# Moving modulation dot products from the retention heads into the later heads, the output projection and the first MLP group

## The chip, the cores and the metric

One core of a Trainium2 chip runs the kernel. The metric is the device time of one execution in microseconds (us), lower is better. Five engines take part: PE multiplies matrices, DVE and ACT work on tiles, POOL does small side work, and SP issues DMAs. Each engine runs its own instructions in order, and they meet through semaphores.

## What is computed

One decoder block for 512 tokens of width 2048, in float32. What matters here is `mod`, six vectors of 2048 that scale, shift and gate the activations. It is one row times a 2048 x 12288 matrix, and only `sh1` and `sc1` are needed by the first norm.

```python
def reference(x, c, w_ada, b_ada, norm1_w, norm2_w, w_in, ...):
    silu_c = jax.nn.silu(c)
    for l in range(DEPTH):
        mod = silu_c @ w_ada[l] + b_ada[l]
        sh1, sc1, g1, sh2, sc2, g2 = jnp.split(mod, 6, axis=-1)
        h = modulate(rms_norm(x, norm1_w[l]), sh1, sc1)
        proj = h @ w_in[l]
        rq, rk, rv, rg, dq, dk, dv = jnp.split(proj, split_pts, axis=-1)
        ...   # 8 retention heads make y_ret, 8 differential heads make y_dif
        mixed = jnp.concatenate([y_ret, y_dif], axis=-1).astype(x.dtype) @ w_out[l]
        x = x + g1[:, None, :] * mixed
        h2 = modulate(rms_norm(x, norm2_w[l]), sh2, sc2)
        mlp = jnp.square(jax.nn.relu(h2 @ w_mlp1[l])) @ w_mlp2[l]
        x = x + g2[:, None, :] * mlp
    return rms_norm(x, final_norm_w)
```

## The kernel before

All matrix products run on PE in a split form. A **chunk** is 8 weight blocks of 128 x 128, 512 KB in all. SP loads it from HBM into one of 4 `raw` slots. ACT rounds it into `w_hi` (`round_w`), DVE makes the rest `w_lo = raw - w_hi` (`rest_w`), both in 2 slots, and PE runs 24 matmuls of 512 columns (`split_products`): 16 with `w_hi`, then 8 with `w_lo`. ACT may write `w_hi` of chunk s when PE has finished chunk s-2 (`chunk_done`), SP may load chunk s when `rest_w` of chunk s-4 is done (`lo_ready`).

The stages, in order:

- The first norm, with the 64 dot products that it needs, and 16 chunks of the input projection.
- Retention heads. Phase h projects head h, and beside that finishes head h-1. Phases 1 to 4 and 8 have 6 chunks, phases 5 to 7 have 8. Phase 8 already loads the first differential head.
- Differential phases 9 to 15 with 6 chunks each. The last head is finished beside the first 8 chunks of the output projection.
- The output projection: tiles m = 0 to 3 together in 8 chunks, then tiles 4 to 15 with 2 chunks each. After each tile DVE adds it to `xy` (`residual_out`) and sums squares.
- The second norm, and 8 MLP groups of 32 chunks: 16 "up" chunks (8 tiles, 2 chunks each) and 16 "down" chunks. In group 0 the first four up tiles share chunks 0 to 7 of the group, up tile 4 is chunks 8 and 9, up tile 5 is chunks 10 and 11, and so on; the down chunks are 16 to 31.

The dot products of `mod` run on DVE. One output column of 128 takes two dots of 128 x 1024, one for each half of `silu_c` (`dot_ada`, line 873). Each needs a 512 KB row block of `ada`, which SP loads into a ring of four slots of `ada_sb` when the dot four before is done (`load_ada`, line 323). In before, the 128 dots that the first norm does not need stand in the eight retention phases, 16 in each: `ADA_6` and `ADA_8` say how many pairs follow the `rest_w` of each chunk j of the phase. At a phase's end `modulation_sum` (lines 1065 and 1070) adds the halves and writes 8 columns of `modr`. `modr` has four rows of 16 columns: gate 1 (used from the output projection's first `residual_out`), shift 2 and scale 2 (used at the second norm), gate 2 (used by the `residual` of the MLP's down tiles).

Nothing plans the order: what each engine does is written out by hand, and SP's queue is one list in which a DMA that has to wait holds up all that stand behind it.

Of the kernel before, what the change touches and what calls it, by code (L numbers as in the profile page):

```python
# [152 lines left out]
def block_kernel(nc, x_t, c, ada, weights, vecs, lams, rot, decay, ident_in, mask_in, out):  # L153
    with ExitStack() as ctx:
        def sb(name, shape, dt=F32):
            return ctx.enter_context(nc.sbuf_tensor(name, shape, dt))
# [100 lines left out]
        relu = sb("relu", [P128, 2, TOK])  # L257
        usq = sb("usq", [P128, 2, TOK])

        bank = [ctx.enter_context(nc.psum_tensor(f"bank{i}", [P128, TOK], F32)) for i in range(8)]  # L260
# [6 lines left out]
        raw_landed = [sem(f"raw_landed{i}") for i in range(NRAW)]  # L267
        ada_landed = [sem(f"ada_landed{i}") for i in range(NADA_1)]
        x_landed = [sem(f"x_landed{i}") for i in range(KT // 2)]
        hi_ready, lo_ready, chunk_done = sem("hi_ready"), sem("lo_ready"), sem("chunk_done")  # L270
# [37 lines left out]
        def _(sp):  # L308
# [9 lines left out]
            def load_ada(a):  # L318
# [4 lines left out]
                sp.dma_start(ada_at(r), ada[a.value()]).then_inc(ada_landed[r], 16)  # L323

            def load_phase(h, s0, slots):

                part = 0
                for j in range(len(slots)):
                    load_raw(s0 + (j + 2))
                    for _ in range(2 * slots[j]):  # L330
                        load_ada(Count(A_RET - 16 + part, (16, h)) if not isinstance(h, int)
                                 else Count(A_RET - 16 + 16 * h + part))
                        part += 1
                    if j == 2 and (not isinstance(h, int) or h < NRET):
                        sp.wait_ge(strips_ready, h)
                        sp.dma_start(decay_sb[:], decay[h]).then_inc(decay_landed, 16)
# [18 lines left out]
            load_phase(NRET, Count(C_DIF), ADA_6)  # L355
            with sp.Fori(0, 10) as i:
                for j in range(4):
                    load_raw(Count(C_DIF + 8 + j, (4, i)))
            for s in range(C_OUT, C_OUT + 12):
                if s >= C_OUT + 4:  # L360
                    p = s - C_OUT - 4
                    sp.wait_ge(act_ready, KT + 2 * p + 2)
                    sp.dma_start(xy[:, 2 * p:2 * p + 2], x_t[:, 2 * p:2 * p + 2]).then_inc(x_landed[p], 16)
                load_raw(Count(s))
            with sp.Fori(0, (N_CHUNKS - C_OUT - 12) // 4) as i:
                for j in range(4):
                    load_raw(Count(C_OUT + 12 + j, (4, i)))
            for tb in range(TB):
# [493 lines left out]
        def _(dve):  # L862
# [198 lines left out]

            def modulation_sum(n, col):

                dve.wait_ge(dot_done, 16 * n + A_RET)
                nc.vector.tensor_tensor(sumr[:], partr[:, :, 0], partr[:, :, 1], ALU.add).then_inc(modr_summed, 1)
                dve.wait_ge(modr_summed, n)
                flat = modr[:].rearrange("p a b -> p (a b)")
                to = flat[:, bass.ds(col, 8)] if not isinstance(col, int) else flat[:, col:col + 8]
                bias = vec[:, bass.ds(col + V_B, 8)] if not isinstance(col, int) else vec[:, V_B + col:V_B + col + 8]
                nc.vector.tensor_tensor(to, sumr[:], bias, ALU.add).then_inc(modr_ready, 1)  # L1070

            def head_ret(h, s0, slots, dif=False):

                part = 0
                for j in range(len(slots)):
                    if j == 1:
                        means_of_v(h - 1)
                    rest_w(s0 + (j + 1))
                    if j == 0:
                        rest_v(h - 1)  # L1080
                    if j == 1:
                        if not isinstance(h, int) or h > 1:
                            finish_ret(h - 2)
                    if j == 2:
                        rotate_q(h, s0 + 2, dif)
                    if j == 4:
                        var_eps(h - 1)
                        rotate_k(h, s0 + 4, dif)
                    for _ in range(slots[j]):
                        a = Count(A_RET - 16 + 16 * h + 2 * part) if isinstance(h, int) else \  # L1090
                            Count(A_RET - 16 + 2 * part, (16, h))
                        modulation_rest(a, part)
                        part += 1
                    if j == 0:
                        decay_strips(h - 1)
                modulation_sum(h, 8 * h - 8)

            def head_dif(h, s0):

                for j in range(6):  # L1100
# [13 lines left out]
                    if j == 2:  # L1114
                        combine(h - 1)
                        rotate_q(h, s0 + 2, True)
                    if j == 4:
                        clamp_o(h - 1)
                        rotate_k(h, s0 + 4, True)
                    if j == 5:  # L1120
                        var_eps(h - 1)

            nc.vector.memset(ones[:], 1.0).then_inc(const_ready, 1)
# [55 lines left out]
            dve.wait_ge(modr_ready, NRET)  # L1179
            nc.vector.scalar_tensor_tensor(amul[:, 1], modr[:, 2], 1.0, vec[:, V_N2:V_N2 + KT], ALU.add, ALU.mult)\  # L1180
                .then_inc(scale_ready, 1)
            head_dif(NRET + 1, Count(C_DIF + 6))
# [55 lines left out]
            for g in range(1, 4):  # L1238
                for t in range(4):
                    for half in range(2 if (g, t) != (1, 0) else 1):  # L1240
                        rest_w(Count(C_OUT + 8 * g + 2 * t + half + (1 if (g, t) != (1, 0) else 2)))
                    m = 4 * g + t
                    residual_out(m, Count(C_OUT + 2 * m + 2))
                    sum_square(KT + m)
            token_mean(2)
            token_diag(2)
# [235 lines left out]
```

## Time and profile before

| | us |
|---|---|
| median of 3 runs | 2445.53 |
| lowest and highest | 2444.48 and 2446.52 |
| span of the profiled execution | 2444.3 |
| PE busy, of the span | 2337.2 |
| DVE busy, of the span | 1280.3 |
| ACT busy, of the span | 750.8 |

The page gives the profiled execution by its span alone; it lies 1.2 us under the median. PE is the engine that is nearly always busy, so the places to look at are those where it is not, or where its clock is down. [...]

### The profile page before, as it was taken

What the parts mean: (1) busy time and instruction counts of PE and PEld (TensorE: products, weight loads), DVE (VectorE), ACT (ScalarE), POOL (GpSimd) and SP (SyncE); (2) the same over time, 40 slices, a digit from 0 to 9 for tenths busy, and PEclk for the clock granted to TensorE, in tenths of its full rate; (3) what the DMA queues carried; (4) which work ended last, traced back from release to release, by engine and by line L of the source; (5) the groups of instructions that cost most, each with busy time, mean ns of one, the idle gap of its engine ahead of it and who ended that gap; (6) DMA issues with size and microseconds to landing.
All of it is one profiled execution on the core that took longest, in us unless ns stands there. A gap on an engine that the chain in (4) does not pass through costs nothing.

```text
span 2444.3 us, 28432 instructions
## 1 busy us (share of the span) xinstructions
PE 2337.2 (96%) x10284; PEld 1895.6 (78%) x10284; DVE 1280.3 (52%) x1752; ACT 750.8 (31%) x1014; POOL 185.0 (8%) x121
## 2 busy tenths in 40 slices
PE   4999999989999999899999999999999999999996
PEld 2567778877777778788888888888888888888885
DVE  7979999885666643443333333333333333333354
ACT  3233333434444532332222221221221221322332
POOL 0013233222122100000000000000000000000000
PEclk9999899999999999899999999999999999999998
DMA  9957777842222422222232223222222232222222
GB/s 369 384 208 272 264 263 263 281 161 77 78 77 69 137 95 94 78 95 95 95 103 95 94 97 100 94 94 96 101 95 94 95 101 97 94 94 99 94 91 86
DMA packets 98308, 328.22 MB, mean 134 GB/s; under 512 B 10064, under 2 KB 18768, under 8 KB 98128
## 3 DMA queue, kind: packets, MB, share of 16 engines
q1 hardware_dynamic: 97248, 326.41, 39.1%
q10 hardware_dynamic: 1008, 1.13, 0.1%
q8 instruction: 31, 0.51, 0.1%
q14 instruction: 21, 0.17, 0.0%
HBM read 323.31 MB, written 4.19 MB: 134 GB/s over the span
## 4 chain that ended last, share of the span: by engine, by line
issue 60%; PE 21%; DVE 12%; ACT 5%; DMA 0%; POOL 0%; DVEq 0%; ACTq 0%; POOLq 0%; SPq 0%
PE bank L389 6%; PE bank L390 6%; PE bank L393 6%; DVE ada_sb L873 4%; DVE w_lo L866 2%; ACT w_hi L621 2%; PE bank L496 1%; ACT prob L705 1%; DVE prob L873 1%; DVE bank L1020 1%; ACT L695 1%; PE bank L412 1%; DVE prob L1048 1%; PE bank L487 0%; ACT prob L688 0%
## 5 line engine op out<-in xcount | busy, mean ns | idle before, releaser
L389 PE MATMUL bank<-act_hi,w_hi 128*128 128x512 f32 x2112 | 842.1, 399 | 16.3 <-DVE act_lo L918 7.8
L390 PE MATMUL bank<-act_lo,w_hi 128*128 128x512 f32 x2112 | 832.7, 394 | 0.0
L866 DVE TENSOR_TENSOR w_lo<-raw,w_hi 128x1024 fp32r<-128x1024 f32 x392 | 495.2, 1263 | 400.9 <-ACT w_hi L621 386.3
L621 ACT ACTIVATE w_hi<-raw 128x1024 fp32r<-128x1024 f32 x392 | 414.3, 1057 | 924.5 <-PE bank L393 874.5
L393 PE MATMUL bank<-act_hi,w_lo 128*128 128x512 f32 x2112 | 521.8, 389 | 0.0
L389 PEld LDWEIGHTS bank<-act_hi,w_hi 128*128 128x128 f32 x2112 | 403.7, 191 | 109.6 <-issue 21.9
L390 PEld LDWEIGHTS bank<-act_lo,w_hi 128*128 128x128 f32 x2112 | 403.1, 191 | 85.0 <-issue 1.7
L393 PEld LDWEIGHTS bank<-act_hi,w_lo 128*128 128x128 f32 x2112 | 396.5, 188 | 82.5
L389 PE MATMUL bank<-u_hi,w_hi 128*128 128x512 f32 x1024 | 399.9, 390 | 0.0
L390 PE MATMUL bank<-u_lo,w_hi 128*128 128x512 f32 x1024 | 398.6, 389 | 0.0
L1227 DVE SCALAR_TENSOR_TENSOR xy<-bank,modr,xy 128x512 f32 (+1 forms) x144 | 108.1, 751 | 434.1 <-PE bank L393 434.1
L393 PE MATMUL bank<-u_hi,w_lo 128*128 128x512 f32 x1024 | 252.9, 389 | 0.0
L873 DVE CUSTOM_DVE_ANT_0 ada_sb<-ada_sb,silu_c 128x1024 f32<-128x1024 f32 x172 | 239.1, 1433 | 0.0
L393 PEld LDWEIGHTS bank<-u_hi,w_lo 128*128 128x128 f32 x1024 | 192.2, 188 | 39.9
L389 PEld LDWEIGHTS bank<-u_hi,w_hi 128*128 128x128 f32 x1024 | 192.3, 188 | 39.8
L390 PEld LDWEIGHTS bank<-u_lo,w_hi 128*128 128x128 f32 x1024 | 192.2, 188 | 39.7
L1262 DVE TENSOR_TENSOR usq<-relu 128x512 f32<-128x512 f32 x64 | 44.3, 692 | 235.2 <-ACT relu L820 235.2
L1318 POOL TENSOR_TENSOR tok_r<-tok_v,minus_half 128x4 f32<-128x4 f32 x3 | 3.9, 1293 | 1582.6 <-DVE tok_v L895 1582.6
L820 ACT ACTIVATE relu<-bank 128x512 f32<-128x512 f32 x64 | 38.2, 598 | 273.4 <-PE bank L393 273.4
L639 ACT ACTIVATE sq<-xy 128x512 f32<-128x512 f32 x48 | 30.1, 630 | 130.5 <-DVE xy L1227 125.9
L412 PE MATMUL bank<-xy,raw 128*128 128x512 f32 x128 | 56.8, 596 | 9.0 <-ACT xy L632 9.0
L1323 POOL TENSOR_TENSOR q_lo<-rot_a,q_hi 128x512 fp32r<-128x512 f32 x16 | 22.7, 1416 | 421.0 <-ACT q_hi L654 421.0
(130 smaller groups left out, 1224.1 us busy)
## 6 DMA issues: line engine op xcount, KB each, us to landing
raw<-weights SPq DMA_DIRECT2D x400, 512.0 KB, 3.3
ada_sb<-ada SPq DMA_DIRECT2D x172, 512.0 KB, 5.0
prob<-ada SPq DMA_DIRECT2D x20, 512.0 KB, 6.5
xy<-x_t SPq DMA_DIRECT2D x16, 512.0 KB, 5.9
out<-xy SPq DMA_DIRECT2D x4, 1024.0 KB, 9.1
decay_sb<-decay SPq DMA_DIRECT2D x7, 256.0 KB, 4.7
silu_c<-c_row SPq DMA_DIRECT2D x1, 1024.0 KB, 5.3
rot_sb<-rot ACTq DMA_DIRECT2D x2, 256.0 KB, 6.9
```

The source lines that it names most:

```text
L389: pe.matmul(acc[:], stationary, hi, start=first, stop=False)
L390: pe.matmul(acc[:], stationary, lo, start=False, stop=False)
L393: mm = pe.matmul(acc[:], w_lo[:, w, i * P128:(i + 1) * P128], hi, start=False, stop=last)
L412: mm = pe.matmul(bank[i][:], raw[:, k % NRAW, i * P128:(i + 1) * P128], xy[:, k], start=k == 0, stop=k == KT - 1)
L496: mm = pe.matmul(ps_a[:, jb * P128:], v_tok[:, jb], strips[:, STRIP[jb]:STRIP[jb] + TOK - jb * P128], start=(jb == 0), stop=(jb == TB - 1) ...
L621: nc.scalar.activation(w_hi[:, w], raw[:, r], ACT.Copy).then_inc(hi_ready, 1)
L639: nc.scalar.activation(sq[:, m % 2], xy[:, m % KT], ACT.Square).then_inc(sq_ready, 1)
L820: nc.scalar.activation(relu[:, t % 2], bank[t][:], ACT.Relu).then_inc(relu_ready, 1)
L866: nc.vector.tensor_tensor(w_lo[:, w], raw[:, r], w_hi[:, w].bitcast(F32), ALU.subtract).then_inc(lo_ready, 1)
L873: nc.vector.tensor_tensor_reduce(ada_at(r), ada_at(r), silu_c[:, half * HALF:(half + 1) * HALF], 1.0, 0.0, ALU.mult, ALU.add, to).then_inc ...
L1227: nc.vector.scalar_tensor_tensor(to, bank[t][:], gate_col, to, ALU.mult, ALU.add).then_inc(bank_free[t], 1)
L1262: nc.vector.tensor_tensor(usq[:, t % 2], relu[:, t % 2], relu[:, t % 2], ALU.mult).then_inc(usq_ready, 1)
```

## The change

Four dots in every phase from 1 to 15, two after chunk 3's `rest_w` and two after the last chunk's (60 dots; the sum at the end of each phase gives 2 columns). Four after each of the output projection's tiles 4 to 12 (36 dots, summed once at tile 13 with the 18 columns, where `amul` for the second norm is now made). The last 32, which make gate 2, use a ring of two slots `late` in the part of SBUF that the heads have left: four dots after each of the up tiles 4 to 7 of MLP group 0, and two after each of that group's first eight down tiles. `silu_c` is kept past the heads for it. SP's list changes to match: in the phases it loads 4 row blocks instead of 16, in the output projection four after every second chunk's load, and in MLP group 0 two behind each chunk load from chunk 9 on.

```diff
+A_UP = A_RET + 96
+NLATE = 2
+ADA_6 = (0, 0, 0, 1, 0, 1)
+ADA_8 = (0, 0, 0, 1, 0, 0, 0, 1)
...
+            def load_late(a):
+
+                r = ada_place(Count(a))[0]
+                if a < A_UP + NLATE:
+                    sp.wait_ge(o_done, NRET + NDIF)
+                else:
+                    sp.wait_ge(dot_done, a + 1 - NLATE)
+                sp.dma_start(late[:, r], ada[a]).then_inc(late_landed[r], 16)
...
+            for s in range(C_OUT + 2, C_OUT + 2 * KT):
...
                 load_raw(Count(s))
-            with sp.Fori(0, (N_CHUNKS - C_OUT - 12) // 4) as i:
+                m = (s - C_OUT - 4) // 2
+                if (s - C_OUT) % 2 == 0 and 4 <= m < 13:
+                    for e in range(4):
+                        load_ada(Count(A_RET + 60 + 4 * (m - 4) + e))
+            late_next = A_UP
+            for s in range(C_MLP, C_MLP + 28):
+                load_raw(Count(s))
+                if s >= C_MLP + 9 and late_next < N_ADA:
+                    for _ in range(2):
+                        load_late(late_next)
+                        late_next += 1
...
+            def modulation_late(col):
+
+                for e in range(2):
+                    a = A_UP + 2 * col + e
+                    r, landed = ada_place(Count(a))
+                    dve.wait_ge(late_landed[r], 16 * landed)
+                    nc.vector.tensor_tensor_reduce(late[:, r], late[:, r], silu_c[:, e * HALF:(e + 1) * HALF], 1.0, 0.0,
+                                                   ALU.mult, ALU.add, partr[:, col % 8, e:e + 1]).then_inc(dot_done, 1)
...
                     residual_out(m, Count(C_OUT + 2 * m + 2))
                     sum_square(KT + m)
+                    if m < 13:
+                        for e in range(2):
+                            modulation_rest(Count(A_RET + 60 + 4 * (m - 4) + 2 * e), 2 * (m - 4) + e)
...
-            up_quad(0, 1, Count(C_MLP + 8))
-            down_group(Count(C_MLP + 16))
+            for t in range(4):
+                for half in range(2):
+                    rest_w(Count(C_MLP + 9 + 2 * t + half))
+                rest_u(0, 4 + t, t)
+                modulation_late(2 * t)
+                modulation_late(2 * t + 1)
+            modulation_sum(NRET + NDIF + 1, 48, 8, A_UP + 16)
+            for m in range(KT):
+                rest_w(Count(C_MLP + 17 + m))
...
+                residual(3, m, m % 4, Count(C_MLP + 17 + m))
+                if m < 8:
+                    modulation_late(8 + m)
```

DVE at the end of retention phase 1, before: `rest_w` of the last chunk, four dots, the sum, then `rest_w` and `v_lo` (`rest_v`) of the next phase. An ISA row with `ada_sb` is a dot, the row `partr` behind it reads its sum.

```order
L866 TENSOR_TENSOR w_lo<-raw,w_hi 128x1024 [waits hi_ready]
L873 ISA ada_sb,partr<-ada_sb,silu_c 128x1024 [waits ada_landed0]
L873 ISA partr 128x1
L873 ISA ada_sb,partr<-ada_sb,silu_c 128x1024 [waits ada_landed1]
L873 ISA partr 128x1
L873 ISA ada_sb,partr<-ada_sb,silu_c 128x1024 [waits ada_landed2]
L873 ISA partr 128x1
L873 ISA ada_sb,partr<-ada_sb,silu_c 128x1024 [waits ada_landed3]
L873 ISA partr 128x1
L1065 TENSOR_TENSOR sumr<-partr 128x8 [waits dot_done]
L1070 TENSOR_TENSOR modr<-sumr,vec 128x8 [waits modr_summed]
L866 TENSOR_TENSOR w_lo<-raw,w_hi 128x1024 [waits hi_ready]
```

The same place after.

```order
L895 TENSOR_TENSOR w_lo<-raw,w_hi 128x1024 [waits hi_ready]
L902 ISA ada_sb,partr<-ada_sb,silu_c 128x1024 [waits ada_landed2]
L902 ISA partr 128x1
L902 ISA ada_sb,partr<-ada_sb,silu_c 128x1024 [waits ada_landed3]
L902 ISA partr 128x1
L1103 TENSOR_TENSOR sumr<-partr 128x2 [waits dot_done]
L1109 TENSOR_TENSOR modr<-sumr,vec 128x2 [waits modr_summed]
L895 TENSOR_TENSOR w_lo<-raw,w_hi 128x1024 [waits hi_ready]
L1000 TENSOR_TENSOR v_lo<-bank,v_hi 128x512 [waits v_hi_ready]
```

Two dots stand there instead of four. In MLP group 0 SP's queue was a loop of chunk loads that wait for `lo_ready` alone. After, from the output projection's last chunks on (the row with x13 ends with chunk 9 of the group), it is this list, in which the first pair of `late` is followed by chunk 10, the second by chunk 11, the third by chunk 12:

```order
L324 DMA raw<-weights 128x1024 [waits lo_ready] x13
L340 DMA late<-ada 128x1024 [waits o_done] x2
L324 DMA raw<-weights 128x1024 [waits lo_ready]
L340 DMA late<-ada 128x1024 [waits dot_done] x2
L324 DMA raw<-weights 128x1024 [waits lo_ready]
L340 DMA late<-ada 128x1024 [waits dot_done] x2
L324 DMA raw<-weights 128x1024 [waits lo_ready]
```

So from chunk 11 on every chunk load stands behind two loads that wait for dots. DVE in the same stretch, from the `rest_w` of chunks 9 and 10 on; `usq` and `u_lo` are `rest_u` of up tile 4, which waits until PE has finished chunk 9:

```order
L895 TENSOR_TENSOR w_lo<-raw,w_hi 128x1024 [waits hi_ready] x2
L1317 TENSOR_TENSOR usq<-relu 128x512 [waits relu_ready]
L1320 TENSOR_TENSOR u_lo<-usq,u_hi 128x512 [waits u_hi_ready,usq_ready]
L1097 ISA late,partr<-late,silu_c 128x1024 [waits late_landed0]
L1097 ISA partr 128x1
L1097 ISA late,partr<-late,silu_c 128x1024 [waits late_landed1]
L1097 ISA partr 128x1
L1097 ISA late,partr<-late,silu_c 128x1024 [waits late_landed0]
L1097 ISA partr 128x1
L1097 ISA late,partr<-late,silu_c 128x1024 [waits late_landed1]
L1097 ISA partr 128x1
L895 TENSOR_TENSOR w_lo<-raw,w_hi 128x1024 [waits hi_ready] x2
```

The first two dots that the second pair of loads waits for come behind `rest_u` of up tile 4; before, `rest_w` of chunk 11 stood there.

## Rows read from the trace of the kernel before

**Rows 1.** PE's waits for `v_lo`: us in total, times, longest us.

```profile
PE bank L441 <- DVE v_lo L971: 13.0, 5, 3.1
```

**Rows 2.** Stretches: length; busy PE, PEld, DVE, ACT, POOL; clock; DMA share; GB/s.

```profile
196.05:240.45 44.40, 41.25 (x176) 33.83 (x174) 42.08 (x59) 14.53 (x20) 13.46 (x8) 0.92 0.78 267
...
329.05:384.35 55.30, 52.17 (x224) 42.85 (x222) 48.42 (x67) 19.83 (x25) 15.01 (x8) 0.94 0.77 268
384.35:433.44 49.09, 49.09 (x223) 40.46 (x222) 44.64 (x61) 19.83 (x25) 13.30 (x7) 1.00 0.78 262
```

**Rows 3.** PE in order of time (start, us): the stall in phase 2.

```profile
201.21 0.47 PE L441 MATMUL bank<-ident_r,v_hi 128*128 128x128 f32 x1 [3.15 <-DVE v_lo L971]
```

**Rows 4.** DVE in order of time: third of four dots, then what PE waits for.

```profile
195.15 1.62 DVE L873 CUSTOM_DVE_ANT_0 ada_sb<-ada_sb,silu_c 128x1024 f32<-128x1024 f32 x1
...
199.34 1.22 DVE L866 TENSOR_TENSOR w_lo<-raw,w_hi 128x1024 fp32r<-128x1024 f32 x1
200.47 0.68 DVE L971 TENSOR_TENSOR v_lo<-bank,v_hi 128x512 fp32r<-128x512 f32 x1
```

**Rows 5.** Stretches from PE's resumption to the end of its lower clock.

```profile
149.14:152.60 3.46, 3.46 (x8) 2.71 (x9) 1.34 (x3) 2.78 (x4) 1.28 (x1) 0.51 1.02 398
201.21:207.20 5.99, 5.99 (x18) 5.12 (x19) 5.96 (x12) 1.14 (x4) 0.00 (x0) 0.50 1.01 402
...
529.35:534.85 5.50, 5.50 (x22) 4.51 (x23) 3.11 (x12) 2.71 (x8) 0.00 (x0) 0.50 0.20 61
```

**Rows 6.** DVE from phase 8's third last-chunk dot to phase 9's first maxima.

```profile
519.66 1.62 DVE L873 CUSTOM_DVE_ANT_0 ada_sb<-ada_sb,silu_c 128x1024 f32<-128x1024 f32 x1
...
524.04 1.22 DVE L866 TENSOR_TENSOR w_lo<-raw,w_hi 128x1024 fp32r<-128x1024 f32 x1
...
527.65 0.17 DVE L1026 TENSOR_SCALAR ntop<-top 128x4 f32<-128x4 f32 x1
```

**Rows 7.** PE at the second scores of phases 9 and 10.

```profile
529.35 0.58 PE L462 MATMUL bank<-k_hi,q_hi 64*128 64x256 f32 x2 [6.79 <-ACT prob L705]
...
573.32 0.39 PE L462 MATMUL bank<-k_hi,q_hi 64*128 64x256 f32 x2 [1.24 <-ACT prob L705]
```

**Rows 8.** DVE in a differential phase, behind the places of the new dots.

```profile
594.36 1.22 DVE L866 TENSOR_TENSOR w_lo<-raw,w_hi 128x1024 fp32r<-128x1024 f32 x1 [2.16 <-ACT w_hi L621]
...
608.86 1.47 DVE L866 TENSOR_TENSOR w_lo<-raw,w_hi 128x1024 fp32r<-128x1024 f32 x1 [5.02 <-ACT w_hi L621]
```

**Rows 9.** Output projection: one tile's two chunks on PE, then DVE in it.

```profile
897.89:908.77 10.88, 10.88 (x50) 9.01 (x49) 3.89 (x4) 2.64 (x3) 0.00 (x0) 1.00 0.29 96
...
900.55 1.22 DVE L866 TENSOR_TENSOR w_lo<-raw,w_hi 128x1024 fp32r<-128x1024 f32 x1 [0.26 <-ACT w_hi L621]
```

**Rows 10.** A dot on DVE, and SP's two loads that wait for it and the next.

```profile
159.54 1.22 DVE L873 CUSTOM_DVE_ANT_0 ada_sb<-ada_sb,silu_c 128x1024 f32<-128x1024 f32 x1
...
160.79 1.47 SPq L323 DMA_DIRECT2D ada_sb<-ada  x2
```

**Rows 11.** MLP group 0: PE starts chunk 10, DVE's `rest_u`, PE starts chunk 11.

```profile
1075.97 0.39 PE L389 MATMUL bank<-act_hi,w_hi 128*128 128x512 f32 x1
...
1077.54 0.69 DVE L1265 TENSOR_TENSOR u_lo<-usq,u_hi 128x512 fp32r<-128x512 f32 x1
...
1081.41 0.39 PE L389 MATMUL bank<-act_hi,w_hi 128*128 128x512 f32 x1
```

**Rows 12.** SP in phase 6: two dot loads and the chunk load behind them.

```profile
412.87 1.48 SPq L323 DMA_DIRECT2D ada_sb<-ada  x2
414.61 0.33 SPq L316 DMA_DIRECT2D raw<-weights  x1
```

**Rows 13.** Issue to landing, us: that chunk load, then one alone at 1079.81.

```profile
raw<-weights SPq DMA_DIRECT2D x1, 512.0 KB, 5.5
...
raw<-weights SPq DMA_DIRECT2D x1, 512.0 KB, 3.4
```

**Rows 14.** The page: `w_hi`'s group, busy us and mean ns of one.

```profile
L621 ACT ACTIVATE w_hi<-raw 128x1024 fp32r<-128x1024 f32 x392 | 414.3, 1057 | 924.5 <-PE bank L393 874.5
```

More of the change, by code:

```diff
@@ L128, in ada_place @@
         return a.base % NADA_1, a.base // NADA_1 + 1
+    if not a.terms and a.base >= A_UP:
+        return (a.base - A_UP) % NLATE, (a.base - A_UP) // NLATE + 1
     return a.place(NADA), a.value(NADA, 1 + -(-A_RET // NADA_1) - A_RET // NADA)
@@ L258, in block_kernel @@
         usq = sb("usq", [P128, 2, TOK])
+        late = sb("late", [P128, NLATE, HALF])
         bank = [ctx.enter_context(nc.psum_tensor(f"bank{i}", [P128, TOK], F32)) for i in range(8)]
@@ L268, in block_kernel @@
         ada_landed = [sem(f"ada_landed{i}") for i in range(NADA_1)]
+        late_landed = [sem(f"late_landed{i}") for i in range(NLATE)]
         x_landed = [sem(f"x_landed{i}") for i in range(KT // 2)]
@@ L330, in load_phase @@
                     for _ in range(2 * slots[j]):
-                        load_ada(Count(A_RET - 16 + part, (16, h)) if not isinstance(h, int)
-                                 else Count(A_RET - 16 + 16 * h + part))
+                        load_ada(Count(A_RET - 4 + part, (4, h)) if not isinstance(h, int)
+                                 else Count(A_RET - 4 + 4 * h + part))
                         part += 1
-                    if j == 2 and (not isinstance(h, int) or h < NRET):
+                    if j == 2 and (slots is ADA_8 or isinstance(h, int) and h < NRET):
                         sp.wait_ge(strips_ready, h)
@@ L355, in _ @@
             load_phase(NRET, Count(C_DIF), ADA_6)
[L356 to L360, printed above, removed]
+            load_phase(NRET + 1, Count(C_DIF + 6), ADA_6)
+            with sp.Fori(0, 3) as i:
+                for e in range(2):
+                    load_phase(2 * i + (NRET + 2 + e), Count(C_DIF + 12 + 6 * e, (12, i)), ADA_6)
+            for s in range(C_OUT + 2, C_OUT + 2 * KT):
+                if C_OUT + 4 <= s < C_OUT + 12:
                     p = s - C_OUT - 4
@@ L364, in _ @@
                 load_raw(Count(s))
-            with sp.Fori(0, (N_CHUNKS - C_OUT - 12) // 4) as i:
+                m = (s - C_OUT - 4) // 2
[9 more added lines that the diff above has]
+                        late_next += 1
+            with sp.Fori(0, (N_CHUNKS - C_MLP - 28) // 4) as i:
                 for j in range(4):
-                    load_raw(Count(C_OUT + 12 + j, (4, i)))
+                    load_raw(Count(C_MLP + 28 + j, (4, i)))
             for tb in range(TB):
@@ L1089, in head_ret @@
                     for _ in range(slots[j]):
-                        a = Count(A_RET - 16 + 16 * h + 2 * part) if isinstance(h, int) else \
-                            Count(A_RET - 16 + 2 * part, (16, h))
-                        modulation_rest(a, part)
+                        rest_of_phase(h, part)
                         part += 1
@@ L1116, in head_dif @@
                         rotate_q(h, s0 + 2, True)
+                    if j == 3:
+                        rest_of_phase(h, 0)
                     if j == 4:
@@ L1121, in head_dif @@
                         var_eps(h - 1)
+                        rest_of_phase(h, 1)
+                modulation_phase(h)
             nc.vector.memset(ones[:], 1.0).then_inc(const_ready, 1)
@@ L1244, in _ @@
                     sum_square(KT + m)
+                    if m < 13:
+                        for e in range(2):
+                            modulation_rest(Count(A_RET + 60 + 4 * (m - 4) + 2 * e), 2 * (m - 4) + e)
+                    if m == 13:
+                        modulation_sum(NRET + NDIF, 30, OUT_COLS, A_UP)
+                        dve.wait_ge(modr_ready, NRET + NDIF)
+                        nc.vector.scalar_tensor_tensor(amul[:, 1], modr[:, 2], 1.0, vec[:, V_N2:V_N2 + KT], ALU.add, ALU.mult)\
+                            .then_inc(scale_ready, 1)
             token_mean(2)
```

37 lines of the change are left out of this document (22 added, 15 removed).

## The prediction

> **What bounds the kernel now.** PE is busy for 2337 of 2444 us, so I looked for where it is not. The list of waits has, for PE, five waits for `v_lo` of 13.0 us in total, the longest 3.1 [rows 1]. The stretches show where they cost. Phase 2 (6 chunks) lasts 44.40 us with DVE busy for 42, and phases 3 and 4 are like it; phase 5 (8 chunks) lasts 55.30. Phase 6 has as many chunks as phase 5, lasts 49.09, and PE never rests in it [rows 2]. So four phases in a row lose the same amount, and their clock column says that part of it is PE at half clock.
>
> PE in order of time shows the stall: 3.15 us, to 201.21, for `v_lo` [rows 3]. On DVE `v_lo` stands behind a `rest_w` and behind the last four dots of the phase before [rows 4]. Phases 2 to 5 each have this stall. A fifth place is phase 9: PE waits 6.79 us for the softmax of the first differential head, where phase 10 waits 1.24 [rows 7], because the maxima on DVE stand behind the last four dots of phase 8 [rows 6]. Between these places and in the MLP, PE runs chunks of 5.44 us back to back [rows 11]. DVE is the bound at five places, each time behind dots.
>
> **Part 1: 96 of 128 dots leave phases 1 to 8.** What counts is the last group of a phase, two dots now instead of four. The third dot began at 195.15 [rows 4]; there DVE now goes on to the sum (0.3), `rest_w` (1.22) and `v_lo` (0.68) and ends at 197.4. PE gets there at 201.21 - 3.15 = 198.06. The wait goes, with 0.7 us to spare. What a phase lasts without it comes from phase 6 less two chunks: 49.09 - 2 x 5.44 = 38.21. Phases 2, 3 and 4 give back 44.4 - 38.2 = 6.2 us each (6.1 to 6.2), and phase 5 gives 55.30 - 49.09 = 6.2: **24.6 us** together, low clock included. PE itself is what is late next.
>
> In phase 9 two dots less take 519.66 to 523.4 away, 3.8 us, and I estimate that what precedes them ends 1 us sooner, since fewer dots stand ahead of an earlier `rest_w` too. The maxima come at 522.8 instead of 527.65, and PE resumes 1.7 us later (as 527.65 to 529.35 now) [rows 6, 7], at 524.5 instead of 529.35. The wait falls from 6.8 to 2.0. [...]
>
> **Part 2: two pairs of dots in each of phases 9 to 15.** A pair takes 2.3 us (its two loads are issued 1.14 apart [rows 10]). The second pair falls into 5.02 us in which DVE is idle, the first into 2.16 [rows 8], so the next `rest_w` comes 0.15 late, and PE needs it some 3.6 us into its chunk: 0. Without that cover each pair would cost up to its 2.3 us.
>
> **Part 3: four dots after each of nine output tiles.** DVE is busy for 3.89 of a tile's 10.88 us, and free at 900.55 - 0.26 = 900.3 [rows 9]. Four dots end at 904.9, `rest_w` at 906.1. PE wants that `w_lo` for the chunk that starts at 897.89 + 5.44 = 903.33, after 16 of its 24 matmuls (3.6), at 906.96. It is covered by 0.9 us: 0. SP holds nothing up here: the four row blocks are asked for when the chunk loads are three chunks ahead.
>
> **Part 4: MLP group 0, where the cost is.** SP's queue is in order. The load of chunk 11 now stands behind the second pair of `late` loads. They wait for the first two late dots, and those stand behind `rest_u` of up tile 4, which waits for the end of chunk 9. Call the start of chunk 10 (1075.97) [rows 11] zero.
>
> DVE ends `rest_u` at 1077.54 + 0.61, so at 2.2. A load is issued 1.25 us after the start of the dot that it waits for (159.54 to 160.79) [rows 10] and the next 1.14 later: 3.4 and 4.6. The chunk load follows at 4.95. How long it takes, the same burst in phase 6 tells: two row blocks 1.15 apart and then the chunk [rows 12], which landed 5.5 us after its issue [rows 13], 414.61 + 5.5 - 412.87 = 7.2 after the first. I take this 7.2 and get a landing at 10.6. `w_hi` takes 1.06 [rows 14]: 11.7. Now chunk 11 starts at 1081.41 - 1075.97 = 5.44. PE waits **6.3 us**.
>
> [...]
>
> Chunk 12 lands at 16 and is wanted at 19.5, so it is in time. But chunk 13 stands behind the dots of up tile 5 as chunk 11 behind those of tile 4, chunk 15 behind tile 6's, chunk 17 behind tile 7's. Four times 8.7 is **34.8 us**. The bounds of one: a chunk load that lands as if alone, after 3.4 us [rows 13], makes the wait 4.0; one that lands 0.8 later than that [rows 13] (an estimate of mine for what the spread of such bursts can be) 7.1. [...]
>
> [...]
>
> In the first eight down tiles each chunk load also stands behind two dots. `residual` and the dots bring the load's issue to 3.9 after a chunk's start, it lands at 9.4, `w_hi` is there at 10.5, wanted two chunks on at 10.88. That is 0.4 of cover, and `rest_w` then presses on `residual`, so it can turn into a wait of 0.2 to 0.6 a chunk: I take **1.5 us** (0 to 5).
>
> **The sum.** -24.6 - 6.5 + 34.8 + 1.5 = +5.2 us. On the span, 2444.3 + 5.2 = 2449.5; the median lies 1.2 above the span, so 2450.7. A gain of 31 and a loss of 36 nearly cancel, which is why I don't trust the sign far.
>
> **The rivals.**
> - *The burst lands fast.* The stretch of phase 6 moves 262 GB/s at a DMA share of 0.78 [rows 2], an output tile's, which is like the MLP's, 96 at 0.29 [rows 9]. If the third load takes 3.4 us, each wait is 2.25 shorter: 2450.7 - 9.0 = 2441.7. Against it: what delays a load in a burst are the two just before it, and these are the same.
> - *SP is not held up*, because the change does not do what I read: then only the gain stays, 2445.5 - 31.1 = 2414.4. The order of the queue and of DVE speaks against it.
> - *The down tiles stall as well.* If a burst lands more than 5.9 us after its issue, the 0.4 of cover is gone in each of eight chunks. At 0.8 more, with `residual` pushed back, a chunk waits 1.2 us: 9.6 instead of 1.5, and the four waits grow by 3.2: 2450.7 + 11.3 = 2462.0. For it: the cover is thin. Against: these waits are too short to bring the clock down, and PE's 1.24 us wait in phase 10 did not.
>
> **How the numbers follow.** What a measurement of this kernel tells from no change is about 0.2%, 4.9 us, so 2440.6 to 2450.4 is "same". The forecast has 0.62 for its own 2446 to 2456, with 0.26 of it under 2450.4; the fast burst 0.18 (2438 to 2446, 0.06 of it under 2440.6); SP free 0.05; the down tiles 0.15. Faster: 0.05 + 0.06 = 0.11. Same: 0.26 + 0.12 = 0.38. Slower: 0.36 + 0.15 = 0.51. The range 2440 to 2460 leaves out SP free, the fast burst's last 0.04 and the down tiles' upper 0.08.
>
> **What would show it.** Phases 2 to 4 at 38.2 us with the clock at 1.00, no wait for `v_lo` over 0.3; phase 9's wait for softmax near 2. The output projection unchanged, with `rest_w` behind the dots. In MLP group 0 four waits of PE of about 6.3 us at chunks 11, 13, 15 and 17, ended by `w_hi`, which ends its own by a DMA; the queue's own wait ended by a late dot; low clock behind each. The forecast is wrong if these waits are absent or well under 4 us, or if new waits stand in the output projection or at chunks 18 to 25.

## The result and the profile after

| | before | after |
|---|---|---|
| median, us | 2445.68 (4 runs) | 2478.38 (4 runs) |
| lowest and highest | 2444.48 and 2446.52 | 2473.66 and 2479.99 |
| ratio, 95% interval | | 1.0131 (1.0119 to 1.0143) |
| span of the profiled execution | 2444.3 | 2471.9 |

The changed kernel is 32.7 us slower by the medians; the forecast was +5.2. The profiled execution is the fastest of its four runs, and its span is 27.6 us longer. I account for these 27.6.

**The retention phases gave what was forecast.** In the changed kernel PE's list of waits up to 440 us has one wait for `v_lo` left, at 159.25 in phase 1, where the kernel before has the same 0.7 us; the four of about 3 us are gone:

```profile
PE bank L470 <- DVE v_lo L1000: 0.7, 1, 0.7
```

The first two stretches below are one period of the loop, phase 2 cut at another point than in [rows 2], 6 chunks, before and then after; the third is phase 5 of after, 8 chunks, cut in the same way. Columns as in [rows 2]; the clock is the granted one, as a share of full speed.

```profile
202.98:247.24 44.26, 41.25 (x176) 33.83 (x176) 41.94 (x59) 14.53 (x20) 13.32 (x7) 0.92 0.78 272
```

```profile
198.35:236.49 38.14, 38.14 (x177) 31.45 (x176) 26.23 (x35) 14.54 (x20) 10.98 (x7) 1.00 0.40 145
...
312.77:361.79 49.02, 49.02 (x225) 40.45 (x224) 25.23 (x37) 19.82 (x25) 10.26 (x7) 1.00 0.39 135
```

After the change PE is busy from end to end, at a clock of 1.00, with DVE busy for 26 us where it was for 42. At the end of phase 5 the changed kernel is 25.3 us ahead.

**Phase 9 gave less.** DVE, POOL and PE in order of time, after (a fence for each):

```profile
490.76 2.30 DVE L902 CUSTOM_DVE_ANT_0 ada_sb<-ada_sb,silu_c 128x1024 f32<-128x1024 f32 x1
...
493.66 2.34 DVE L895 TENSOR_TENSOR w_lo<-raw,w_hi 128x1024 fp32r<-128x1024 f32 x1
...
498.39 0.17 DVE L1055 TENSOR_SCALAR ntop<-top 128x4 f32<-128x4 f32 x1
```

```profile
492.07 1.48 POOL L1412 TENSOR_SCALAR rs<-rs 128x512 f32<-128x512 f32 x1
493.63 1.29 POOL L1414 TENSOR_TENSOR rs<-rs 128x512 f32<-128x512 f32 x1
```

```profile
500.10 0.58 PE L491 MATMUL bank<-k_hi,q_hi 64*128 64x256 f32 x2 [3.10 <-ACT prob L734]
```

The last dot ends at 493.06, and `rest_w` behind it takes 2.34 us where it took 1.22 before [rows 6]: it now falls beside a tensor operation of POOL. The wait is 3.10 instead of 6.79 us [rows 7].

**From there to the MLP nothing changes.** These two stretches run from phase 9 to the start of chunk 10 of MLP group 0, before and after: 28 + 36 = 64 dots more on DVE (365 us busy instead of 291), and 530.3 us in both.

```profile
545.66:1075.97 530.31, 506.75 (x2331) 408.13 (x2330) 291.22 (x481) 215.34 (x354) 72.87 (x55) 0.98 0.27 88
```

```profile
516.67:1047.02 530.35, 506.16 (x2332) 408.03 (x2330) 364.93 (x626) 215.46 (x354) 73.01 (x55) 0.98 0.43 146
```

**In MLP group 0 PE waits four times.** PE's waits over the whole run, then PE at the four, then SP and ACT at the first, and the landing of that chunk load (issue to landing, us):

```profile
PE bank L418 <- ACT w_hi L650: 24.2, 4, 7.0
...
PE bank L491 <- ACT prob L734: 12.2, 8, 3.1
```

```profile
1047.02 0.39 PE L418 MATMUL bank<-act_hi,w_hi 128*128 128x512 f32 x1
...
1058.56 0.80 PE L418 MATMUL bank<-act_hi,w_hi 128*128 128x512 f32 x1 [5.95 <-ACT w_hi L650]
1077.22 0.80 PE L418 MATMUL bank<-act_hi,w_hi 128*128 128x512 f32 x1 [5.61 <-ACT w_hi L650]
1096.80 0.80 PE L418 MATMUL bank<-act_hi,w_hi 128*128 128x512 f32 x1 [5.66 <-ACT w_hi L650]
1116.70 0.79 PE L418 MATMUL bank<-u_hi,w_hi 128*128 128x512 f32 x1 [6.98 <-ACT w_hi L650]
```

```profile
1050.45 1.47 SPq L340 DMA_DIRECT2D late<-ada  x2
1051.97 0.43 SPq L324 DMA_DIRECT2D raw<-weights  x1
```

```profile
1057.46 1.06 ACT L650 ACTIVATE w_hi<-raw 128x1024 fp32r<-128x1024 f32 x1 [8.97 <-DMA raw<-weights]
```

```profile
raw<-weights SPq DMA_DIRECT2D x1, 512.0 KB, 5.5
```

Low clock follows each wait; the first two such stretches (behind the other two it was 0.52 and 0.50):

```profile
1058.56:1062.57 4.01, 4.01 (x9) 3.14 (x10) 1.21 (x1) 0.00 (x0) 0.00 (x0) 0.50 0.70 253
1077.22:1083.25 6.03, 6.03 (x14) 4.74 (x15) 1.67 (x2) 1.06 (x1) 0.00 (x0) 0.51 0.44 171
```

Compared chunk by chunk with before, the four places cost 33.7 us with their low clock.

**And then the MLP's down chunks are longer, all of them.** A group's 16 down chunks are 384 long matmuls on `u_hi` and `u_lo`, its 16 up chunks 384 on `act_hi` and `act_lo`. One down stretch of before, then a down and an up stretch of after:

```profile
1630.85:1717.89 87.04, 87.04 (x385) 72.07 (x384) 32.26 (x33) 18.11 (x18) 0.00 (x0) 1.00 0.29 96
```

```profile
1644.40:1734.36 89.96, 89.96 (x385) 72.32 (x384) 32.26 (x33) 18.11 (x18) 0.00 (x0) 1.00 0.29 93
1734.36:1821.44 87.08, 87.08 (x385) 72.07 (x384) 30.06 (x31) 24.85 (x30) 0.00 (x0) 1.00 0.29 96
```

PE waits for nothing, its clock is 1.00, the other engines do the same work: but a matmul follows the one before it after 89.96 / 384 = 234.3 ns, not after 226.7. Eight such stretches are 8 x 2.92 = 23.4 us. Together: -25.3 - 3.7 + 33.7 + 23.4 = 28.1, which is 0.5 more than the span shows. The last group's down matmuls account for it: they are 1.9 us longer than before, not 2.9.

### The profile page after: what moved, and what is told of

Same layout as the page of the kernel before. It is cut to its first block, busy times and chain, and to the rows that moved or that the text cites. A ratio compares the mean times of both kernels' runs of the same rounds, so it can differ in the third digit from the quotient of the medians.

```text
span 2471.9 us, 28194 instructions
## 1 busy us (share of the span) xinstructions
PE 2355.7 (95%) x10284; PEld 1892.9 (77%) x10284; DVE 1254.6 (51%) x1772; ACT 751.2 (30%) x1014; POOL 164.5 (7%) x121
## 4 chain that ended last, share of the span: by engine, by line
issue 62%; PE 25%; DVE 8%; ACT 4%; DMA 0%; POOL 0%; DVEq 0%; ACTq 0%; POOLq 0%; SPq 0%
PE bank L418 7%; PE bank L419 7%; PE bank L422 7%; DVE ada_sb L902 2%; PE bank L525 1%; ACT w_hi L650 1%; DVE w_lo L895 1%; ACT prob L734 1%; DVE prob L902 1%; DVE bank L1049 1%; PE bank L441 1%; DVE prob L1077 1%; ACT L724 0%; PE bank L516 0%; ACT prob L717 0%
## 5 line engine op out<-in xcount | busy, mean ns | idle before, releaser
L418 PE MATMUL bank<-u_hi,w_hi 128*128 128x512 f32 x1024 | 408.4, 399 | 7.0 <-ACT w_hi L650 7.0
L419 PE MATMUL bank<-u_lo,w_hi 128*128 128x512 f32 x1024 | 406.8, 397 | 0.0
L422 PE MATMUL bank<-u_hi,w_lo 128*128 128x512 f32 x1024 | 260.6, 396 | 0.0
L902 DVE CUSTOM_DVE_ANT_0 ada_sb<-ada_sb,silu_c 128x1024 f32<-128x1024 f32 x140 | 175.3, 1295 | 0.0
L441 PEld LDWEIGHTS bank<-xy,raw 128*128 128x128 f32 x128 | 24.4, 194 | 38.4 <-issue 38.2
```

What stands on the lines that cost most here:

```text
L418: pe.matmul(acc[:], stationary, hi, start=first, stop=False)
L419: pe.matmul(acc[:], stationary, lo, start=False, stop=False)
L422: mm = pe.matmul(acc[:], w_lo[:, w, i * P128:(i + 1) * P128], hi, start=False, stop=last)
L441: mm = pe.matmul(bank[i][:], raw[:, k % NRAW, i * P128:(i + 1) * P128], xy[:, k], start=k == 0, stop=k == KT - 1)
L902: nc.vector.tensor_tensor_reduce(ada_at(r), ada_at(r), silu_c[:, half * HALF:(half + 1) * HALF], 1.0, 0.0, ALU.mult, ALU.add, to).then_inc ...
```

## Why the down chunks are longer: the experiments

No instruction of the down chunks differs between the kernels. What differs is where `u_hi` and `u_lo` lie in SBUF. The built program gives each tensor's start address. `partr` and `sumr` have grown (64 to 144 bytes and 32 to 72 in each partition), and `tok_v` behind them starts at 150912 instead of 150752, 160 bytes higher; `silu_c` (8192 bytes) now lies ahead too, so `u_hi` and `u_lo` start 160 + 8192 = 8352 bytes higher. Start addresses as they stand in the two built programs, bytes in a partition:

```
          before   after            before   after
w_hi       32896   32896   act_hi    49280   49280
w_lo       41088   41088   act_lo    82048   82048
u_hi      169344  177696   u_lo     185728  194080
```

All of before are multiples of 64 (and of 128); 177696 is 32 past one. That was my first theory. The kernels that test it compute everything, and differ by padding alone. Behind each median stand, in brackets, the ratio to the kernel before as it was measured beside it and its 95% interval; differences given with a sign are to that median.

### First theory: the moving operand must start at a multiple of 64 bytes

`a_pad32` is the changed kernel, `b_pad32` and `b_pad64` the kernel before, with 8, 8 and 16 floats in this place:

```diff
+        pad = sb("pad", [P128, 8])
         tok_v = sb("tok_v", [P128, TB])
```

**a_pad32.** 

> The changed kernel with a tensor of 8 floats put ahead of the token buffers, so that u_hi and u_lo start at multiples of 64 bytes in SBUF again, as in the kernel before; they still lie 8 KB higher than there, and no instruction is moved. Theory (where the moving operand starts within 64 bytes sets the pace of its matmuls): the 128 MLP-down chunks go back from 5.62 to 5.44 us, 128 x 0.183 = 23.4 us less than the changed kernel, about 2455 us, 9 us slower than the kernel before; the four waits of PE for w_hi in MLP group 0 stay (some 34 us). Rival (the place 8 KB higher in SBUF, silu_c's move, or how late work stands on VectorE makes those chunks long): no change, 2478 us.

Measured: 2475.61 us (1.0119, 1.0102 to 1.0135). Only 2.8 us less.

**b_pad32.** 

> The kernel before with 8 floats put ahead of the token buffers and u_hi, u_lo: these then start 32 bytes past a multiple of 64. Not one instruction differs otherwise. Theory (start of the moving operand): all 128 MLP-down chunks last 5.62 instead of 5.44 us, +23.4 us, about 2469 us. Rival (it is the changed order of work, not the address): 2445.7 us, no change.

Measured: 2464.92 us (1.0080, 1.0064 to 1.0097), +19.2 where 23.4 were expected. So 32 bytes of padding and nothing else slow the kernel before: the cause is the address, not the moved dots.

**b_pad64.** 

> The kernel before with 16 floats (64 bytes) put there: every later tensor moves, but u_hi and u_lo keep starting at multiples of 64 bytes. Theory (start within 64 bytes): no change, 2445.7 us. Rival (any shift of these tensors against the others, or another larger unit such as 128 or 256 bytes): up to +23 us, 2469 us.

Measured: 2452.51 us (1.0028, 1.0018 to 1.0038), +6.8. The theory's 0 is out; the rival, which said up to 23, holds.

**b_w32**, the kernel before with 8 floats ahead of `w_hi` and 8 ahead of `act_hi`. 

> The kernel before with only w_hi and w_lo, the operands that are loaded into TensorE as weights, 32 bytes past a multiple of 64; everything behind them is padded back. Theory (only the moving operand's start counts, weight loads lie beside the matmuls): no change, 2445.7 us. Rival (any operand of the matmul off the 64 bytes lengthens it): all 392 chunks get longer, by 0.18 us each, +72 us, about 2517 us.

Measured: 2491.94 us (1.0185, 1.0168 to 1.0202), +46.2. The theory is refuted, but my kernel was not clean: the second padding left `act` and `u` 64 bytes past a multiple of 128.

**b_act32**, 8 floats ahead of `act_hi` and 8 ahead of `xy`. 

> The kernel before with only act_hi and act_lo, the moving operands of the projections and of the MLP-up chunks, 32 bytes past a multiple of 64; u_hi, u_lo and the rest keep their addresses. Theory (start of the moving operand): the 128 up chunks last 5.62 instead of 5.44 us, 128 x 0.183 = 23.4 us, and the 128 projection chunks as much longer where PE bounds them, so +23 to +47 us, 2469 to 2492 us; the down chunks stay at 5.44. Rival (something only in the down chunks): no change, 2445.7 us.

Measured: 2477.23 us (1.0128, 1.0111 to 1.0145), +30.8: inside the theory's range, yet its down chunks, which should have stayed, took 87.89 us for 16.

**b_u16**, with `u_hi` and `u_lo` made 64 bytes larger and used from their fifth float on. 

> The kernel before with u_hi and u_lo 16 bytes past a multiple of 64. One more 64-byte piece per row of 2048 bytes (33 in place of 32, 226.7 x 33/32 = 233.8 ns) is touched here as well as at 32 bytes: by that theory the down chunks last 5.62 us, +23.4 us, 2469 us. Rival (the unit is 16 bytes, or the cost grows with the offset): 0 to +12 us, 2446 to 2457 us.

Measured: 2456.98 us (1.0037, 1.0022 to 1.0051), +10.5. The extra 64 bytes had also moved `u_lo` by 80 in all, so the 16 bytes were not tested alone. The time is at the upper end of the rival's range, but with the two operands at different places it doesn't decide between the two.

### Second theory: a multiple of 128 bytes

**a_pad96**, the changed kernel with 24 floats instead of 8. 

> The changed kernel with 24 floats (96 bytes) of padding, so that u_hi and u_lo start at multiples of 128 bytes, as all operands of the long matmuls do in the kernel before; they lie 8 KB higher than there all the same. No instruction is moved. Theory (a multiple of 128 bytes is what counts, 64 was too little): the matmuls on u_hi and u_lo go from 234.2 back to 226.9 ns, 128 chunks x 0.18 = 23 us less than the changed kernel, about 2455 us. Rival (the place 8 KB higher, or the late work itself, makes them long, as padding by 32 bytes alone brought only 233.3 ns): no change, 2476 to 2478 us.

Measured: 2457.62 us (1.0052, 1.0035 to 1.0068), 20.8 less than the changed kernel, where 23 were expected. In its profiled execution the four waits cost 38.5 us with their low clock, 4.8 more than in the changed kernel's. The down stretch is back:

```profile
1641.33:1728.37 87.04, 87.04 (x386) 72.10 (x385) 32.26 (x33) 18.14 (x18) 0.00 (x0) 1.00 0.29 96
```

Three more kernels are the kernel before with padding ahead of `u_hi` alone (2048, 2064 and 2096 floats):

```diff
         heads.close()
 
+        pad = sb("pad", [P128, 2048])
         u_hi = sb("u_hi", [P128, BLOCKS, TOK], F32R)
```

**b_8k.** 

> The kernel before with 8 KB put ahead of u_hi, u_lo, relu and usq alone; all stay on multiples of 128 bytes, and nothing else moves. Theory (128 bytes): no change, 2446 us, 226.9 ns per matmul. Rival (the place, 8 KB higher): 233 ns, +18 to +23 us, 2464 to 2469 us.

Measured: 2446.32 us (1.0002, 0.9993 to 1.0012). The place 8 KB higher does not matter.

**b_8k64.** 

> The kernel before with 8 KB and 64 bytes put ahead of u_hi, u_lo, relu and usq alone: they start 64 bytes past a multiple of 128. 64 bytes alone gave 229 ns in the kernel before, and 8 KB with 64 bytes gave 233.3 ns in the changed kernel. If the offset within 256 bytes is what tells these two apart (192 there, 64 here), this one, with 192, gives 229 ns, +7 us, 2453 us; if the place 8 KB higher does, it gives 233 ns, +19 us, 2465 us; if only multiples of 64 were needed, 2446 us.

Measured: 2452.78 us (1.0026, 1.0016 to 1.0036), 16 down chunks in 87.91 us, as in `b_pad64`.

**b_8k192.** 

> The kernel before with 8 KB and 192 bytes put ahead of u_hi, u_lo, relu and usq alone: these have exactly the addresses that they have in the changed kernel with 8 floats of padding (64 bytes past a multiple of 256), where their matmuls took 233.3 ns. Theory (the start within 256 bytes sets the pace, 64 there against 192 in the earlier run with 229 ns): 233.3 ns here too, 128 chunks x 0.153 = +19.6 us, 2465 us. Rival (64 past a multiple of 128 gives 229 ns at either place, and what makes the rest in the changed kernel is its late work or its other tensors, 32 bytes off): 229 ns, +7 us, 2453 us.

Measured: 2465.23 us (1.0078, 1.0062 to 1.0095). So 64 and 192 bytes past a multiple of 256 differ, and the late work has no part in it:

```profile
1640.52:1730.12 89.60, 89.60 (x386) 71.81 (x384) 32.26 (x33) 18.06 (x18) 0.00 (x0) 1.00 0.28 94
```

**b_w32c**, the clean form of `b_w32`: 8 floats ahead of `w_hi`, 24 ahead of `act_hi`. 

> The kernel before with w_hi and w_lo alone 32 bytes past a multiple of 128; everything behind them is padded on to the next multiple of 128, so that act_hi, act_lo, u_hi and u_lo, the moving operands, are aligned (in the earlier run with these weights they stood 64 bytes off, which took 233 ns). Theory (only the moving operand counts): 226.9 ns, 2446 us. Rival (the operand loaded as weights counts as well): 230 to 234 ns in all long matmuls, +30 to +60 us, 2476 to 2506 us.

Measured: 2489.91 us (1.0183, 1.0166 to 1.0200), +45.0, in the rival's range. All moving operands stand on multiples of 128, and both kinds of stretch are long, so the weights' address counts:

```profile
1653.28:1742.88 89.60, 89.60 (x385) 72.08 (x384) 32.27 (x33) 18.13 (x18) 0.00 (x0) 1.00 0.28 94
1742.88:1832.48 89.60, 89.60 (x385) 72.08 (x384) 30.06 (x31) 24.86 (x30) 0.00 (x0) 1.00 0.28 94
```

### What stands: the distance between the two operands, modulo 256 bytes

**b_all32**, the kernel before with 8 floats ahead of `w_hi` and no other padding. 

> The kernel before with 8 floats put ahead of w_hi: every tensor behind raw moves by 32 bytes, so that w, act and u keep their distances to each other, and all start 32 bytes past a multiple of 128. Theory (each operand's own start counts): 233 to 240 ns in all long matmuls, +45 us or more, about 2490 us. Rival (the distance of the two operands counts, modulo 128 or 256 bytes): 226.9 ns, 2446 us.

Measured: 2447.21 us (1.0002, 0.9993 to 1.0012). The rival holds: no long matmul's operand is at a multiple of 64, and the pace is that of before.

```profile
1631.69:1718.73 87.04, 87.04 (x385) 72.09 (x384) 32.26 (x33) 18.18 (x18) 0.00 (x0) 1.00 0.29 96
```

**b_u128**, with 32 floats ahead of `u_hi` alone. 

> The kernel before with 128 bytes put ahead of u_hi, u_lo, relu and usq alone. In all kernels with 226.9 ns so far, both operands stood 128 past a multiple of 256; here u_hi and u_lo stand at a multiple of 256 and the weights do not. Theory (multiples of 128 bytes suffice): 226.9 ns, 2446 us. Rival (the two must agree modulo 256, or lie at 128): 229 to 233 ns on u_hi and u_lo, +7 to +20 us, 2453 to 2466 us.

Measured: 2465.49 us (1.0074, 1.0057 to 1.0091). The rival holds again; both operands at multiples of 128 is not enough.

```profile
1639.12:1728.72 89.60, 89.60 (x386) 72.08 (x384) 32.25 (x33) 18.11 (x18) 0.00 (x0) 1.00 0.28 94
```

Both forms of my theory, each operand's own start, have fallen. `b_pad32` and `b_all32` show it best. In both `u_hi` starts at 169376 and `u_lo` at 185760, and only the weights differ, at 32896 or at 32928; yet the down stretch of `b_pad32` is

```profile
1638.38:1727.98 89.60, 89.60 (x385) 71.96 (x384) 32.26 (x33) 18.10 (x18) 0.00 (x0) 1.00 0.29 94
```

where `b_all32` has 87.04. By the start addresses in their built programs, all kernels sort by the start of the moving operand less the start of the weights, modulo 256:

| distance | 16 chunks, us | ns per matmul | seen in |
|---|---|---|---|
| 0 | 87.04 | 226.7 | before, a_pad96, best96, sp96, dve96, b_8k, b_all32 |
| 16 (u_hi), 80 (u_lo) | 88.53 | 230.5 | b_u16 |
| 32 | 89.60 | 233.3 | b_pad32, b_w32, up chunks of b_act32 |
| 64 | 87.9 | 228.9 | b_pad64, b_8k64, down chunks of b_act32 |
| 96 | 89.60 | 233.3 | b_w32c |
| 128 | 89.60 | 233.3 | b_u128 |
| 160 | 89.96 | 234.3 | after, a_fix |
| 192 | 89.60 | 233.3 | a_pad32, best, b_8k192 |

A unit of 128 bytes is excluded by `b_u128`. One of 512 is excluded too: `u_hi` starts 136448 bytes behind `w_hi` in the kernel before, 256 past a multiple of 512, and 144896 bytes in `a_pad96`, a multiple of 512, and both have 87.04. A shift of both operands together was tried for 32 bytes only.

With the weights alone moved by 32 bytes (`b_pad32` against `b_all32`) the matmuls of the down chunks follow each other after 233.3 or 226.7 ns. What in the chip makes this pace, no run shows. The table is a description of float32 matmuls of 512 columns with a weight load beside each, and its rows between the tried distances are open.

## The four waits: SP's order, DVE's order, or both

`a_fix` (no padding), `best` (8 floats) and `best96` (24 floats) are the changed kernel with two edits in MLP group 0: SP issues all pairs but the first three chunk loads later (the second behind chunk 13's load instead of chunk 10's; the texts on record say four), and DVE makes two of a tile's four dots right after the tile's first `rest_w` and only two after `rest_u`.

```diff
-                if s >= C_MLP + 9 and late_next < N_ADA:
+                if (s == C_MLP + 9 or s >= C_MLP + 13) and late_next < N_ADA:
...
-                for half in range(2):
-                    rest_w(Count(C_MLP + 9 + 2 * t + half))
-                rest_u(0, 4 + t, t)
+                rest_w(Count(C_MLP + 9 + 2 * t))
                 modulation_late(2 * t)
+                rest_w(Count(C_MLP + 10 + 2 * t))
+                rest_u(0, 4 + t, t)
                 modulation_late(2 * t + 1)
```

**a_fix.** 

> The changed kernel, u_hi and u_lo left where it puts them, with the late work of MLP group 0 spread out: SyncE issues its later pairs of modulation-weight loads four chunk loads later, so that none of them stands ahead of a chunk load that PE soon needs, and VectorE takes them one per chunk and not two together. Theory (the two causes add): PE's four waits for w_hi of some 7 us with their low clock go, -34 us, about 2444 us; the down chunks keep their 5.62 us. Rival (the waits come from elsewhere, such as VectorE's order or the load of the DMA queues): they stay, 2478 us, or come at other chunks.

Measured: 2439.41 us (0.9974, 0.9964 to 0.9984), 39.0 less than the changed kernel where 34 were expected. Its list of waits has none for `w_hi` in the MLP.

**best.** 

> The changed kernel with both mended: the 8 floats of padding, and the late work of MLP group 0 spread out. Theory (two separate causes, and retention's gain is real): -23.4 and -34 us from 2478, so about 2420 us, 26 to 29 us faster than the kernel before. Rival (the gain in retention is taken back later once the two causes are gone): about 2446 us.

Measured: 2437.29 us (0.9963, 0.9951 to 0.9976). The time was missed, since 8 floats were the wrong padding (distance 192, 8 x 2.56 = 20.5 us of the 23.4 left in). That the waits are gone was met.

**best96.** 

> The changed kernel with the late work of MLP group 0 spread out and the 24 floats of padding. Theory (128 bytes; the causes add): 2437.3 us, the time with 8 floats of padding, less 23, about 2414 to 2417 us, some 30 us faster than the kernel before. Rival (place): 2437 us.

Measured: 2419.59 us (0.9896, 0.9880 to 0.9913), 26 us faster than before and 3 us above the expected range. PE from ahead of the first late dot on, at full clock without a pause:

```profile
1035.85:1200.00 164.15, 164.15 (x724) 135.73 (x725) 99.32 (x134) 42.89 (x50) 0.00 (x0) 1.00 0.57 192
```

The gain of the retention phases and phase 9, 29 us, was thus real, and hidden by two costs.

Both edits were made at once there, so each was made alone, on `a_pad96`.

**sp96**, SP's line only. 

> The changed kernel with 24 floats of padding and only SyncE's order changed: the later pairs of modulation-weight loads are issued four chunk loads later; VectorE keeps two dots together after rest_u of an up tile. Theory (the waits come from where the pairs stand in SyncE's queue): the four waits of PE for w_hi of 6 to 7 us go, and at most short ones for w_lo behind two dots stay (0 to 1.3 us at each of four chunks), so 2419 to 2425 us against 2457.6 with the padding alone. Rival (VectorE's pairs of dots make the waits): they stay, 2457 us.

Measured: 2434.10 us (0.9957, 0.9944 to 0.9969). The waits for `w_hi` go, but those for `w_lo` are up to 3.2 us long, not 1.3, and low clock follows (0.59 on average from 1057.79 to 1062). PE at two of the four, then DVE at the first:

```profile
1057.79 3.68 PE L423 MATMUL bank<-act_hi,w_lo 128*128 128x512 f32 x8 [2.53 <-DVE w_lo L896]
1073.70 2.75 PE L423 MATMUL bank<-act_hi,w_lo 128*128 128x512 f32 x8 [3.16 <-DVE w_lo L896]
```

```profile
1052.73 1.23 DVE L1098 CUSTOM_DVE_ANT_0 late<-late,silu_c 128x1024 f32<-128x1024 f32 x1 [2.15 <-DMA late<-ada]
...
1055.37 1.23 DVE L1098 CUSTOM_DVE_ANT_0 late<-late,silu_c 128x1024 f32<-128x1024 f32 x1 [1.40 <-DMA late<-ada]
...
1056.52 2.36 DVE L896 TENSOR_TENSOR w_lo<-raw,w_hi 128x1024 fp32r<-128x1024 f32 x2
```

With two slots the third and fourth dot can't start before their row blocks land, which are asked for when the first two are done. DVE stands at them for 3.55 us, with `rest_w` behind. I had counted the dots' work and not that wait.

**dve96**, DVE's order only. 

> The changed kernel with 24 floats of padding and only VectorE's order changed: one late dot after each rest_w of an up tile in place of two together; SyncE's queue is as in the changed kernel. Theory (the waits come from where the pairs stand in SyncE's queue, behind a dot that VectorE does late): the four waits stay in a similar size, 2450 to 2459 us. Rival (VectorE's pairs make them): they go, 2420 us.

Measured: 2428.91 us (0.9928, 0.9912 to 0.9945). My theory is refuted: it said that the four waits would stay and the time be 2450 or more. SP's first held pair goes out at 1047.22 and the chunk load behind it at 1048.74, 1.8 us ahead of chunk 10's start (1050.57) and not 4.95 behind it, since the dots that it waits for come right after a `rest_w`. Eight short waits for `w_hi` are left, of 0.6 to 1.4 us, and the clock stays at 1.00; the first two:

```profile
1063.20 0.47 PE L419 MATMUL bank<-act_hi,w_hi 128*128 128x512 f32 x1 [1.37 <-ACT w_hi L651]
1075.59 0.47 PE L419 MATMUL bank<-act_hi,w_hi 128*128 128x512 f32 x1 [1.25 <-ACT w_hi L651]
```

So the cause is the two together: a chunk load behind a pair in SP's queue, and that pair held by dots that DVE makes late, after `rest_u`. Either edit alone takes more than half of the four waits' cost away (23.5 and 28.7 of the 38.0 us between `a_pad96` and `best96`).

## Where the prediction was right and where wrong

- **Part 1, phases 2 to 5.** 24.6 forecast, 25.3 measured; 38.21 us a phase forecast, 38.14 measured. Right.
- **Part 1, phase 9.** 6.5 forecast, 3.7 measured. Two steps failed. The maxima were to come 4.85 us sooner and came 4.0 sooner (498.39 against 527.65 - 25.25), since the dots' gap puts `rest_w` beside POOL. And the 1.6 that the 6.5 holds beyond this was for less low clock behind a shorter wait, an estimate of mine that no run shows; what the runs show in its place is low clock for 6.1 us after 3.10 us of waiting in `after`, and for 5.5 after 6.79 in `before` [rows 5], so nothing came back.

```profile
500.10:506.24 6.14, 6.14 (x23) 5.06 (x24) 4.02 (x13) 3.35 (x12) 0.00 (x0) 0.50 0.47 171
```

- **Parts 2 and 3.** 0 forecast, 0 measured (530.31 and 530.35 us). The cover held.
- **Part 4.** 34.8 forecast, 33.7 measured: 24.2 us of waiting (25.2 forecast, 4 x 6.3) and 9.5 of low clock and restart (9.6). Each 8.7 of the forecast holds 2.4 for the latter, and so does the 19.5 for chunk 12 (11.7 + 5.44 + 2.4), an estimate of mine that no run shows. What the runs showed in its place: in `before` 8 matmuls take 3.46 us at a clock of 0.51 [rows 5], 0.43 each, against 5.44 / 24 = 0.227 back to back in the MLP [rows 11], so about 0.47 of such a stretch is lost, 1.6 us of the one of 3.46 and 2.8 of the one of 5.99; in `after` it is 9.5 / 4 = 2.4 a wait. The places were right, chunks 11, 13, 15 and 17. For the first, the pair's issue came 3.43 us after chunk 10's start (3.4 forecast), the chunk load's at 4.95 (4.95), its landing at 10.4 (10.6). The third load of the burst took 5.5 us, as in phase 6 [rows 13]. The size is right for this execution. From one to another it varies: the four held chunk loads land 5.1 to 6.6 us after their issue here and 6.0 to 6.5 in `a_pad96`, where the four waits come to 27.0 us and cost 38.5.
- **Down tiles 18 to 25.** 1.5 forecast, about 0.3 measured, within the bounds 0 to 5. In `a_pad96` it was 1.8.
- **The rivals.** The fast burst, SP free and stalling down tiles did not come. The sign, slower, was the forecast's, but for the 23.4 us it had no reason.
- **The step that failed is the sum.** It adds -24.6, -6.5, +34.8 and +1.5 and has no term for the storage: `partr` and `sumr` grow and `silu_c` moves ahead of `u_hi`, and I put that at nothing without a reason. So the pace of 5.44 us a chunk, which the prediction reads for the MLP of before, was carried over to all 128 down chunks of after; the runs show 89.96 / 16 = 5.62 there. With a term of 23.4 for it the sum is +28.6, against 27.6 measured. The trace of before had no row from which its size could be read, as all long matmuls there run at one distance; an honest range would have had to say so and reach beyond 2460.

The median of the changed kernel lies 4.7 us above its profiled execution. That part is not traced. The four waits, 4.8 us dearer in `a_pad96`, could be its cause; this is not shown.

## What to carry to other kernels

Here an edit to the buffers slowed matmuls that it did not touch, from 226.7 to 234.3 ns: when a tensor grows or moves, work out where everything behind it starts, keep moving operands and weights of matmuls like these at one offset modulo 256 bytes (the other distances took 228.9 to 234.3 ns), and hold the spacing of matmuls in an untouched loop against the kernel before. In SP's queue a load that waited for a dot held those behind it: in the changed kernel chunk 11's load went out behind its pair, 4.95 us after chunk 10 had begun. Ask when the engine comes to the work waited for, and put the work ahead of its own waits. When a forecast gain seems not to arrive, look for a second cost before doubting the first gain: here 29 us of gain stood behind 57 us of two unrelated costs.

## What the runs showed of the hardware

- A float32 matmul of 512 columns follows the one before it after 226.7 ns where moving operand and weights start at the same offset modulo 256 bytes, and after 228.9 to 234.3 where they don't, with PE's clock at 1.00 and no wait in the stretches (the table above).
- Low clock was not in proportion to the wait ahead of it: in the changed kernel 6.1 us of it followed 3.10 us of waiting, 4.0 us followed 5.95. Waits of 1.1 to 1.4 us in `dve96` left the clock at 1.00, and so did the one of 1.24 us in phase 10 of before [rows 7].
- The same `rest_w` took 1.22 us before and 2.34 us after, the latter beside a tensor operation of POOL; none of the 354 in the changed kernel that have no POOL instruction beside them took over 1.23, and the 38 that have one took 1.21 to 2.34.
